# One-column products to other stages, position statistics spread over a panel, and a different order of work at the norms with a shift

## The chip, the cores and the metric

One core of one Trainium2 chip runs the whole program. The metric is the device time of one execution in microseconds (us); lower is better. TensorE (PE in the rows, its weight loads PEld), VectorE (DVE), ScalarE (ACT), GpSimd (POOL) and SyncE (SP, which issues the loads) each run an instruction stream of their own and meet at semaphores.

## The reference, cut to what matters

A transformer on x of 512 positions by 1024 channels, in float32, four layers in all. Two of them belong to a first block whose norms have a scale and a shift made from a condition vector c:

```python
mods = silu(c) @ ada_w[layer] + ada_b[layer]           # 6 blocks of 1024 per layer
sh1, sc1, g1, sh2, sc2, g2 = split(mods, 6)
h = rms_norm(x, norm_mix_g) * (1 + sc1) + sh1
x = x + g1 * (mixer(h) @ w_out)     # layer 0: LRU and stick-breaking; layer 1: 16 heads, window 128
h = rms_norm(x, norm_ffn_g) * (1 + sc2) + sh2
x = x + g2 * ((silu(causal_conv(h @ w_gate)) * (h @ w_up)) @ w_down)
```

The second block (differential attention, a dilated attention of three groups, two squared-relu MLPs) has norms with a gain only; there `rms_norm(x) @ w` is computed as `(x * gain) @ w`, and the factor `1/rms` of each position is applied to the product.

## The kernel before, in words

x lies transposed in `xT` as 8 chunks of 128 channels by 512 positions. Every float32 product of weight and activation is made from three products of rounded parts: high by high, high by low, low by high. A weight tile comes by DMA into `raw`, ACT rounds it into `whi` (`high`, L1641), POOL takes the difference `wlo` (`split`, L873); tile pairs alternate between two buffers. `steps` (L360 to L455) is the list of stages in program order, and each engine's function walks it: "norm", "gemm" (of kinds panel, ffn, relu, down and so on), "window", "stick", "bar", "mods". A unit of a down stage is 8 or 6 channel chunks, so 24 or 18 matmuls of 512 columns, and adds one chunk to `xT` (`down`, L2341 on DVE).

**Modulation sums.** silu(c) @ ada_w needs 12 blocks of 1024 sums. DVE forms, for each block, a 128 by 1024 partial sum over 8 loaded tiles (`ada_add`, L564/L566), and TensorE adds up over the partitions: for each group of 128 columns one matmul whose weights are the partial sum and whose moving operand is a single column of ones (`products`, L1243). These are the one-column products; each shows as two loads and two matmuls in the trace. Blocks 2 to 4 are added up during the stick attention in bursts of 8. Block 5 (the gate of the first ffn) is added up in the down stage behind it, one product after each of 8 units. Blocks 6 to 11 belong to the second layer: in the three down stages of the first ffn one, two and three products follow each of 8 units. The results gather in PSUM columns (`sum_column`) and `modulation` (L2253, L2258) on DVE adds the bias, as the step "mods".

**A norm with a shift.** Three of them follow a down stage (they begin near 300, 688 and 902 us; the very first, at the program's start, is not touched). While the down stage runs, ACT squares each finished chunk (L1787) and DVE adds the square to `sq_sum` (L2201). After the last unit all of PE, ACT and DVE pass a barrier (`bar`); PE keeps busy with 8 matmuls of no use (`keep_rate`, L973), then multiplies `sq_sum` by ones in float32 (L1198), which gives every partition the sum. Twelve more matmuls of no use follow. ACT rounds the weights of the next stage's second unit (in `norm`, ahead of the sum), takes Ln (L1593) and Exp (L1595); DVE scales chunk after chunk (L2455), ACT adds the shift and rounds (L1822), and the first unit of the next stage starts as chunks come in. Ahead of the barrier at 688 ACT also loads a table (L1569).

**Position statistics.** The second block has two fresh norms in front of panels (near 1283 and 1941 us). There each position's sum of squares is wanted on its own partition, in two orders: `token_stats` on TensorE (L1088) multiplies 128 by 128 blocks of `sq_sum` by one column of ones, four blocks that lie together and four whose columns lie four apart. All 8 are issued in one burst after the first of the panel's four rows of work (`l == 0`); ACT reads them (L1709), then DVE.

**Window attention** (`window`, 776 to 857 us) goes head by head: TensorE computes scores (L1345 to L1348), transposes the probabilities (L1356) and adds values (L1367), with heads overlapped.

## Time and profile before

| | |
|---|---|
| median of 3 runs | 2935.57 us (2933.58 to 2941.92) |
| span of the profiled execution | 2940.3 us |
| TensorE matmul busy | 2841.3 us, 97% |
| TensorE weight load busy | 2319.8 us, 79% |
| DVE, ACT, POOL busy | 1744.2, 1222.0, 1077.7 us |
| mean granted TensorE clock | 0.991 |

The rows give a span only, so the profiled execution's own time is known as its span, 2940.3 us, which is 4.7 us above the median. In a timeline row the first number is the start in us, the second the duration; "x8" is the number of instructions merged; the bracket gives idle time just before and what ended it. A clock of 1.00 is 2.4 GHz and 0.50 is 1.2 GHz.

### The profile page before, as it was taken

To read this page: it belongs to the slowest core of one execution; us is meant where nothing else is said; L and a number is where in the kernel's file an instruction comes from. 1 tells how busy PE (TensorE), PEld (TensorE's weight loads), DVE (VectorE), ACT (ScalarE), POOL (GpSimd) and SP (SyncE) were. 2 spreads that over 40 slices of the span, in tenths; PEclk is the share of its full clock that TensorE was granted. 3 is DMA by queue.
4 is the path that set the end of the run, shared out by engine and by line. 5 is a ranking of instruction groups with operands and counts; after the bars stand their busy time and mean duration, and the time that the engine had idled before them with its cause. 6 is when DMAs were issued, how large, how long until landed. Compare 5 with 4: busy or idle time off the path is not lost.

```text
span 2940.3 us, 38997 instructions
## 1 busy us (share of the span) xinstructions
PE 2841.3 (97%) x13385; PEld 2319.8 (79%) x13396; DVE 1744.2 (59%) x2106; ACT 1222.0 (42%) x2059; POOL 1077.7 (37%) x490
## 2 busy tenths in 40 slices
PE   6999999999899999999889999999999999999999
PEld 5767788887677888888658888888888889888887
DVE  7486776776556554668666334557666766544333
ACT  3574432223554322244453222256556665522221
POOL 1312344443213444444314444444422442244443
PEclk9999999999999999999989999999999999999999
DMA  6255263643112333332003333333201330133332
GB/s 217 86 173 185 84 204 98 207 134 91 36 36 79 93 100 93 93 95 87 29 15 93 93 94 98 95 88 94 87 30 52 88 93 30 51 93 93 99 95 93
DMA packets 366012, 278.96 MB, mean 95 GB/s; under 512 B 13490, under 2 KB 321075, under 8 KB 365875
## 3 DMA queue, kind: packets, MB, share of 16 engines
q1 hardware_dynamic: 364624, 276.83, 31.1%
q8 instruction: 82, 1.34, 0.2%
q14 instruction: 55, 0.45, 0.1%
q10 hardware_dynamic: 1251, 0.33, 0.0%
HBM read 275.03 MB, written 2.10 MB: 94 GB/s over the span
## 4 chain that ended last, share of the span: by engine, by line
PE 67%; DVE 3%; ACT 2%; issue 2%; POOL 0%; DVEq 0%; ACTq 0%; POOLq 0%
PE banks L1158 13%; PE banks L1153 12%; PE banks L1162 12%; PE banks L1022 6%; PE banks L1028 6%; PE banks L1025 6%; PE banks L1427 2%; PE banks L995 1%; PE banks L1367 1%; PE banks L1493 1%; PE banks L1155 1%; PE banks L1356 0%; PE banks L1063 0%; PE banks L1400 0%; PE banks L1401 0%
## 5 line engine op out<-in xcount | busy, mean ns | idle before, releaser
L873 POOL TENSOR_TENSOR w_lo<-w_raw,w_hi 128x1024 fp32r<-128x1024 f32 (+1 forms) x423 | 1027.1, 2428 | 1706.8 <-ACT w_hi L1641 1705.8
L1641 ACT ACTIVATE w_hi<-w_raw 128x1024 fp32r<-128x1024 f32 (+1 forms) x424 | 445.6, 1051 | 1131.3 <-PE banks L1162 799.4
L1022 PE MATMUL banks<-w_hi,h_hi 128*128 128x512 f32 x960 | 387.1, 403 | 1.4 <-ACT h_hi L1822 1.4
L1028 PE MATMUL banks<-w_lo,h_hi 128*128 128x512 f32 x960 | 377.3, 393 | 0.7 <-POOL w_lo L873 0.7
L1025 PE MATMUL banks<-w_hi,h_lo 128*128 128x512 f32 x960 | 376.6, 392 | 0.7 <-DVE h_lo L596 0.7
L1153 PE MATMUL banks<-h_hi,w_hi 128*128 128x512 f32 x1280 | 339.0, 393 | 6.7 <-ACT h_hi L1822 6.7
L1158 PE MATMUL banks<-h_lo,w_hi 128*128 128x512 f32 x1280 | 320.8, 391 | 2.5 <-DVE h_lo L596 2.4
L1153 PEld LDWEIGHTS banks<-h_hi,w_hi 128*128 128x128 f32 x1280 | 240.9, 188 | 63.9 <-issue 8.4
L1158 PEld LDWEIGHTS banks<-h_lo,w_hi 128*128 128x128 f32 x1280 | 240.3, 188 | 57.5 <-DVE h_lo L596 8.3
L1162 PE MATMUL banks<-h_hi,w_lo 128*128 128x512 f32 x1152 | 284.5, 389 | 0.0
L1162 PEld LDWEIGHTS banks<-h_hi,w_lo 128*128 128x128 f32 x1152 | 216.2, 188 | 44.9
L1153 PE MATMUL banks<-mid_hi,w_hi 128*128 128x512 f32 x864 | 220.4, 394 | 8.2 <-ACT mid_hi L1774 4.7
L1028 PEld LDWEIGHTS banks<-w_lo,h_hi 128*128 128x128 f32 x960 | 196.7, 205 | 35.5 <-POOL w_lo L873 1.5
L1022 PEld LDWEIGHTS banks<-w_hi,h_hi 128*128 128x128 f32 x960 | 196.7, 205 | 32.8 <-issue 2.1
L1025 PEld LDWEIGHTS banks<-w_hi,h_lo 128*128 128x128 f32 x960 | 197.3, 206 | 31.9 <-DVE h_lo L596 1.0
L1158 PE MATMUL banks<-mid_lo,w_hi 128*128 128x512 f32 x864 | 218.3, 391 | 2.2 <-DVE mid_lo L2321 2.1
L2338 DVE TENSOR_TENSOR xT<-banks,xT 128x512 f32 (+1 forms) x80 | 55.3, 691 | 268.6 <-PE banks L1162 266.8
L1162 PE MATMUL banks<-mid_hi,w_lo 128*128 128x512 f32 x864 | 214.6, 390 | 0.0
L1153 PEld LDWEIGHTS banks<-mid_hi,w_hi 128*128 128x128 f32 x864 | 160.6, 188 | 46.4 <-ACT mid_hi L1774 8.1
L1158 PEld LDWEIGHTS banks<-mid_lo,w_hi 128*128 128x128 f32 x864 | 162.2, 188 | 41.4 <-DVE mid_lo L2321 4.7
L1162 PEld LDWEIGHTS banks<-mid_hi,w_lo 128*128 128x128 f32 x864 | 162.2, 188 | 33.6
L2331 DVE TENSOR_TENSOR mid_lo<-tmp,mid_hi 128x512 f32 (+1 forms) x64 | 123.9, 1936 | 55.6 <-ACT mid_hi L1774 55.6
(364 smaller groups left out, 4260.6 us busy)
## 6 DMA issues: line engine op xcount, KB each, us to landing
Z<-in_ada_w SPq DMA_DIRECT2D x64, 512.0 KB, 5.0
w_raw<-in_m_w_up SPq DMA_DIRECT2D x64, 512.0 KB, 3.9
w_raw<-in_m_w_down SPq DMA_DIRECT2D x64, 512.0 KB, 3.7
w_raw<-in_kv_w SPq DMA_DIRECT2D x48, 512.0 KB, 3.7
w_raw<-in_ffn_w_gate SPq DMA_DIRECT2D x44, 512.0 KB, 3.7
w_raw<-in_ffn_w_up SPq DMA_DIRECT2D x44, 512.0 KB, 3.7
tmp<-in_ada_w SPq DMA_DIRECT2D x32, 512.0 KB, 4.6
w_raw<-in_ffn_w_down SPq DMA_DIRECT2D x32, 512.0 KB, 3.9
```

The lines of the kernel that those rows point to most:

```text
L873: pool.tensor_tensor(wlo[j][:, 0:n], raw[j][:, 0:n], whi[j][:, 0:n], ALU.subtract).then_inc(s_wlo, 1)
L995: mm = pe.transpose(turned(n)[:, j * P:(j + 1) * P], tmp[4 + n % 2][:, j * P:(j + 1) * P], ident)
L1022: pe.matmul(t, hh, wh, start=k == 0, stop=False)
L1025: pe.matmul(t, hl, wh, start=False, stop=False)
L1028: mm = pe.matmul(t, hh, wl, start=False, stop=k == DC - 1)
L1153: pe.matmul(g, whi[par][:, k * P:(k + 1) * P], hi[:, k * S:(k + 1) * S], start=(k == 0), stop=False)
L1158: mm = pe.matmul(g, whi[par][:, k * P:(k + 1) * P], lo[:, k * S:(k + 1) * S], start=False, stop=early and k == st.kc - 1)
L1162: mm = pe.matmul(g, wlo[par][:, k * P:(k + 1) * P], hi[:, k * S:(k + 1) * S], start=False, stop=(k == st.kc - 1))
L1427: mm = pe.matmul(o, dil_vals[:, at:at + P], dil_probs[q % 2][:, own:own + width], start=g == 0 and c == 0, stop=g == 2 and c == NB - 1, sk ...
L1641: act.activation(whi[par][:, 0:kc * P], raw[par][:, 0:kc * P], ACT.Copy).then_inc(s_whi, 1)
L2331: dve.tensor_tensor(ch(mlo, l), tmp[1], ch(mhi, l), ALU.subtract).then_inc(r_lo, 1)
L2338: dve.tensor_tensor(x, G[par], x, ALU.add).then_inc(evac[par], 1)
```

## The change

1. The 8 products of block 5 leave the down stage after the stick attention and go to the norm behind it: each is followed by one matmul of no use, in place of the 12. Their "mods" step moves behind the first ffn stage.
2. The second down stage of the first ffn has one product per unit in place of two, the third none in place of three. Blocks 8 to 11 are added up in the window attention instead, 8 products in a burst ahead of the scores of heads 2, 5, 8 and 11; their "mods" step (3) stands between the window attention and its barrier. DVE's partial sums for blocks 6 to 11 lie in other tiles, since the window uses four of them; the adds themselves stay where they were. Other PSUM columns hold the results.
3. The position statistics are issued two at a time, after each of the four tiles of the second row (`l == 1`). ACT reads them at `l == 2`; DVE makes the head tables first and waits for them after.
4. At the three norms with a shift DVE no longer adds the last square. TensorE multiplies the sum of seven squares by ones behind the first 8 matmuls of no use, and after the barrier adds ones times the last square.
5. At the same norms ACT rounds the weights of the second unit ahead of the barrier and ahead of the last square, in place of after the barrier.

The diff, with context cut:

```diff
@@ -414,12 +414,12 @@
         steps[-1][1].after_stick = True
-        steps[-1][1].products, steps[-1][1].ada = (0, [3]), (0, 8, 8)
-        steps.append(("mods", 1))
+        steps[-1][1].ada = (0, 8, 8)
         ffn(0)
+        steps.insert(next(n for n, (k, st) in enumerate(steps) if k == "gemm" and st.kind == "ffn") + 1, ("mods", 1))
         downs = [st for k, st in steps if k == "gemm" and st.kind == "down" and st.rhs == "mid"]
-        for st, blocks, ada in zip(downs, ([0], [1, 2], [3, 4, 5]), ((8, 16, 8), (24, 16, 8), (40, 8, 4))):
-            st.products, st.ada = (1, blocks), ada
+        for st, blocks, ada in zip(downs, ([0], [1], None), ((8, 16, 8), (24, 16, 8), (40, 8, 4))):
+            st.products, st.ada = blocks and (1, blocks), ada
         steps.append(("mods", 2))
@@ -428,7 +428,7 @@
         panel(od, D, 8, 256, a["od_kn_g"])
-        steps += [("bar", None), ("window", None), ("bar", None)]
+        steps += [("bar", None), ("window", None), ("mods", 3), ("bar", None)]
         gemm_stage("down", 8, DC, a["od_w_out"][0], "y", gate=48 + 16)
@@ -528,7 +528,7 @@
-            t, o = (bank[6], 2 * P) if FIRST * DC <= c < 5 * DC else (bank[7], 0)
+            t, o = (bank[6], 2 * P) if FIRST * DC <= c < 6 * DC else (bank[7], 0) if c < 8 * DC else (bank[4], 0)
             return t[:, o + c:o + c + n]
@@ -537,7 +537,7 @@
         ada_parts = [dict(blocks=range(FIRST, 6), sums=[zt(2 * b, 2) for b in range(4)], ring=[TMP[:, 2 * j * S:(2 * j + 2) * S] for j in range(4)], before=0),
-                     dict(blocks=range(6, 12), sums=[zt(16 + 2 * b, 2) for b in range(6)], ring=[zt(28 + 2 * j, 2) for j in range(4)], before=32)]
+                     dict(blocks=range(6, 12), sums=[zt(16 + 2 * ((b + 4) % 6), 2) for b in range(6)], ring=[zt(28 + 2 * j, 2) for j in range(4)], before=32)]
@@ -555,7 +555,7 @@
             q = ada_parts[part]
-            t = q["sums"][b] if isinstance(b, int) else zt(2 * b, 2)
+            t = q["sums"][b]
             i = DC * b + k
@@ -972,11 +972,14 @@
-            def bar(waits=0):
+            def bar(waits=0, si=None):
                 flush()
                 keep_rate(waits)
+                if si:
+                    pe.wait_ge(n_add, past((DC + 1) * si - 1))
+                    pe.matmul(bank[2], ones, sq_sum, start=True, stop=False).then_inc(n_add, 1)
                 pe.wait_ge(bar_act, nbar[0])
@@ -1032,6 +1035,8 @@
                             turn(before, 0)
+                        if l == 1 and st.norm.raw and st.norm.fresh and st is first_of(st.norm):
+                            token_stats(st.norm, b)
                         if st.first_pair is not None and l in (1, 2):
@@ -1041,8 +1046,6 @@
                         turn(before, l + 1)
-                    if l == 0 and st.norm.raw and st.norm.fresh and st is first_of(st.norm):
-                        token_stats(st.norm)
                 pending[0] = st if st.normed else None
@@ -1080,13 +1083,14 @@
-            def token_stats(norm):
+            def token_stats(norm, b):
                 pe.wait_ge(n_add, past((DC + 1) * norm.sum_index))
-                for k in range(2 * NB):
+                for k in range(2 * b, 2 * b + 2):
                     block = sq_sum[:, k * P:(k + 1) * P] if k < NB else by_class(sq_sum)[:, k - NB, :]
                     mm = pe.matmul(bank[7][:, k:k + 1], block, ones[:, 0:1], start=True, stop=True)
-                mm.then_inc(n_ss, 1)
+                if b == NB - 1:
+                    mm.then_inc(n_ss, 1)
@@ -1194,9 +1198,14 @@
                 if fresh and si > 1 and not norm_list[ni].raw:
-                    pe.wait_ge(n_add, past((DC + 1) * si))
-                    pe.matmul(bank[2], ones, sq_sum, start=True, stop=True).then_inc(n_ss, 1)
-                    keep_rate(12)
+                    pe.wait_ge(n_sq, past(DC * si))
+                    pe.matmul(bank[2], ones, squares[1], start=False, stop=True).then_inc(n_ss, 1)
+                    if si == 2:
+                        for t in range(DC):
+                            products(0, [3], t, 1)
+                            keep_rate(1)
+                    else:
+                        keep_rate(12)
@@ -1338,6 +1347,8 @@
                     pe.wait_ge(e["probs"], past(h - 2))
+                    if h % 3 == 2 and h < 12:
+                        products(1, [2 + h // 3])
                     for b in range(NB):
@@ -1522,7 +1533,10 @@
                     after = steps[at_step + 1] if at_step + 1 < len(steps) else (None, None)
-                    bar(8 if after[0] == "norm" and not norm_list[after[1][0]].raw and at_step else 0)
+                    if after[0] == "norm" and at_step:
+                        bar(8, after[1][1])
+                    else:
+                        bar()
                 elif kind == "norm":
@@ -1571,7 +1585,9 @@
-            def bar():
+            def bar(wide=None):
+                if wide:
+                    high(DC, 1, wide.base + 1, wide.base // 2)
                 if pending[0]:
@@ -1721,7 +1737,7 @@
                         high(kc, 1 - l % 2, st.base + l + 1, (st.base + l + 1) // 2, *following(st, l + 1))
-                    if l == 0 and st.norm.raw and st.norm.fresh and st is first_of(st.norm):
+                    if l == 2 and st.norm.raw and st.norm.fresh and st is first_of(st.norm):
                         if other_tables[0]:
@@ -1812,7 +1828,7 @@
                     return
-                if nxt.early:
+                if nxt.early and ni == 0:
                     high(DC, 1, nxt.base + 1, nxt.base // 2)
@@ -2147,7 +2163,8 @@
                 if kind == "bar":
-                    bar()
+                    after = steps[at_step + 1:at_step + 3]
+                    bar(after[1][1] if at_step and after and after[0][0] == "norm" and after[1][1].early else None)
                 elif kind == "norm":
@@ -2269,8 +2286,10 @@
                     modulation(5, 6, [])
+                elif part == 2:
+                    modulation(6, 8, [(1, 0)])
                 else:
-                    modulation(6, 12, [(1, 0), (1, 1)])
+                    modulation(8, 12, [(1, 1)])
@@ -2341,7 +2360,7 @@
                         raw_low(st.raw_next, l)
-                    if st.squares is not None:
+                    if st.squares is not None and (st.raw_next or not (isinstance(l, int) and l == st.n - 1)):
                         add_square(st.squares, l, par)
@@ -2430,10 +2449,11 @@
                     pending[0] = None
+                if st.normed:
+                    head_tables(st)
                 if st.norm.raw and st.norm.fresh and st is first_of(st.norm):
                 if st.normed:
-                    head_tables(st)
                     for b in range(NB):
```

## Rows read from the trace of the kernel before

**Rows 1.** The page: busy time of each engine, share of the span, instructions.
```profile
PE 2841.3 (97%) x13385; PEld 2319.8 (79%) x13396; DVE 1744.2 (59%) x2106; ACT 1222.0 (42%) x2059; POOL 1077.7 (37%) x490
```
**Rows 2.** Timeline of PE, down stages with one and with two products a unit.
```profile
266.25 0.28 PE L1243 MATMUL banks<-ones_r,Z 128*128 128x1 f32 x2
271.94 0.28 PE L1243 MATMUL banks<-ones_r,Z 128*128 128x1 f32 x2
...
545.67 0.50 PE L1243 MATMUL banks<-ones_r,Z 128*128 128x1 f32 x4
...
551.62 0.50 PE L1243 MATMUL banks<-ones_r,Z 128*128 128x1 f32 x4
```
**Rows 3.** The chain in order of time, a down stage without products.
```profile
866.17 1.81 PE banks L1158 x8
```
**Rows 4.** Timeline, third down stage of the first ffn, three products a unit.
```profile
668.53 4.25 DVE L564 SCALAR_TENSOR_TENSOR Z<-Z,small 128x1024 f32<-128x1024 f32 x2
...
673.49 1.66 PE L1153 MATMUL banks<-mid_hi,w_hi 128*128 128x512 f32 x6 [1.21 <-DVE xT L2341]
...
678.29 1.63 PE L1153 MATMUL banks<-mid_hi,w_hi 128*128 128x512 f32 x6
```
**Rows 5.** Timeline of PE, window attention at its start and in its middle.
```profile
788.46 0.66 PE L1356 MATMUL banks<-squares,tmp 128*128 128x128 f32 x4 [2.67 <-DVE tmp L2590]
...
805.82 0.31 PE L1345 MATMUL banks<-qk_parts 128*128 128x128 f32 x1
...
810.24 0.31 PE L1345 MATMUL banks<-qk_parts 128*128 128x128 f32 x1
```
**Rows 6.** Stretches (us, busy of PE, PEld, DVE, ACT, POOL, clock, DMA): a stick burst.
```profile
192.30:194.10 1.80, 1.72 (x16) 1.75 (x16) 1.45 (x4) 1.76 (x4) 0.00 (x0) 1.00 0.61 150
194.10:198.00 3.90, 3.90 (x25) 3.20 (x25) 3.68 (x5) 3.38 (x8) 0.00 (x0) 1.00 0.29 100
```
**Rows 7.** Timeline of DVE, the modulation step in front of another barrier.
```profile
252.84 0.18 DVE L2253 TENSOR_TENSOR mods<-banks,params 128x24 f32<-128x24 f32 x1
253.06 0.17 DVE L2258 SCALAR_TENSOR_TENSOR norm_scale<-mods,params 128x8 f32<-128x8 f32 x1
```
**Rows 8.** Timeline, the third norm with a shift.
```profile
902.48 0.75 DVE L2341 SCALAR_TENSOR_TENSOR xT<-banks,mods,xT 128x512 f32<-128x512 f32 x1 [1.29 <-PE banks L1162]
...
902.77 1.67 PE L973 MATMUL banks<-mask_b,ident_b 128*128 128x512 bf16 x7 [0.33 <-issue]
903.26 0.63 ACT L1787 ACTIVATE tmp<-xT 128x512 f32<-128x512 f32 x1 [4.58 <-DVE xT L2341]
903.92 0.69 DVE L2201 TENSOR_TENSOR tmp<-tmp 128x512 f32<-128x512 f32 x1 [0.70 <-ACT tmp L1787]
...
904.74 1.06 ACT L1641 ACTIVATE w_hi<-w_raw 128x1024 fp32r<-128x1024 f32 x1 [0.85 <-DVEq L2186]
904.76 1.10 PE L1198 MATMUL banks<-tmp,ones_r 128*128 128x512 f32 x2 [0.32 <-DVEq L2186]
...
905.69 2.75 PE L973 MATMUL banks<-mask_b,ident_b 128*128 128x512 bf16 x12
...
905.87 2.35 POOL L873 TENSOR_TENSOR w_lo<-w_raw,w_hi 128x1024 fp32r<-128x1024 f32 x1 [5.24 <-ACT w_hi L1641]
905.89 0.69 ACT L1593 ACTIVATE tmp<-banks,small 128x512 f32<-128x512 f32 x1
```
**Rows 9.** All of DVE's L2455 in that norm, ns min/median/max.
```profile
L2455 DVE SCALAR_TENSOR_TENSOR tmp<-xT,norm_scale,rstd x8: 737/740/1400, 907.4 to 912.7; 128x512 f32<-128x512 f32 x8
```
**Rows 10.** Timeline of ACT, the norm near 688 us.
```profile
688.89 1.28 ACT L1569 ACT_TABLE_LOAD   x1
```
**Rows 11.** Timeline of PE, the first burst of position statistics.
```profile
1282.64 2.81 PE L1088 MATMUL banks<-ones_r,tmp 128*128 128x1 f32 x16
```
**Rows 12.** Stretches around that burst, columns as in rows 6.
```profile
1282.60:1285.30 2.70, 2.70 (x17) 2.66 (x16) 0.00 (x0) 0.00 (x0) 0.44 (x1) 1.00 0.32 68
1285.30:1289.00 3.70, 3.70 (x10) 2.95 (x11) 0.98 (x5) 1.63 (x4) 1.74 (x1) 0.54 0.28 101
```

## The prediction

> **What bounds the kernel now.** I read the page first: TensorE is busy 97% of the span [rows 1], so most of the time is the number of matmuls times their pitch, and an edit elsewhere counts only where TensorE waits. Then the timeline of each place that the diff touches. About 0.3% (8.8 us) is what a measurement of this kernel can tell from no change.
>
> A plain down unit is three groups of 8 matmuls at 1.81 us, 5.44 us [rows 3]. With one one-column product behind it the period is 271.94 - 266.25 = 5.69, with two 551.62 - 545.67 = 5.95 [rows 2]: a product costs TensorE 0.25 us although its one column is next to nothing. What it costs are weight loads that no long matmul hides.
>
> The burst of 8 position statistics begins at 1282.64 [rows 11] and holds TensorE for 2.7 us. The clock is 1.00 (2.4 GHz) in it and falls to 0.54, mostly the 1.2 GHz level, for the 3.7 us behind it [rows 12]; TensorE had streamed almost no columns for 2.7 us though its record says busy. The second burst, at 1941 us, does the same.
>
> At a norm with a shift TensorE waits for a chain: last square on ACT, its add on DVE, the float32 sum, Ln, Exp, then DVE's first scaled chunk. That first chunk takes 1400 ns where the others take 740 [rows 9], and POOL's split of the second weight tile runs from 905.87 to 908.22, over its first half [rows 8]. DVE starts a chunk each 0.66 us, so about 0.66 us is lost there.
>
> **Products out of the down stages.** Down stage behind the stick attention: 7 periods shrink by 0.25, -1.75 us (the eighth product lies behind the last unit, in the norm). Second down stage: 8 x (5.95 - 5.69) = -2.1. DVE carries two partial sums a unit there as it does in the first down stage, whose period with one product is 5.69 as well, so it allows that. Third: three products cost a period of 678.29 - 673.49 = 4.80 against 4.08 for 18 matmuls (three quarters of 5.44). But TensorE does not set the pace of the first units: DVE takes 4.25 us for two adds, and TensorE waits 1.21 us for it at 673.49 [rows 4]. That wait grows by what the products leave, so only the units behind it gain: two full periods, 2 x 0.7 = -1.4, not 5.6. No range below 0 for these three; -1.4 could be -3 if DVE's wait is shorter than it looks.
>
> **Products into the window attention.** A stick burst of 8 takes 1.8 us, at clock 1.00 in and behind it [rows 6]. In the middle of the window attention a head starts each 810.24 - 805.82 = 4.42 us with no idle time between its matmuls [rows 5], so three of the four bursts are bought in full: 3 x 1.85 = +5.6. The first, ahead of head 2, meets TensorE's idle 2.67 us before 788.46 [rows 5]. But DVE takes the maxima of head 2 before it scales head 0, which that wait is for, so I charge 0.4. Sum +6.0; bounds 0 (if heads are paced by ACT and DVE after all) and 8.2 (four bursts of 2.05).
>
> **The modulation steps.** The one between window and barrier is two small DVE instructions behind the last output, 252.84 to 253.23 where they stand in the same place now [rows 7]: +0.4, 0 to 0.6. TensorE, ACT and POOL all wait at that barrier. The step behind the first ffn stage costs the same 0.4 on DVE with a down stage's partial sums queued behind it; they have 0.4 us slack in every unit of 5.69, so 0. The one at 688 us gets shorter but stands behind a table load. The new place of DVE's sums costs nothing.
>
> **The three norms.** In the third norm [rows 8] the 8 filler matmuls end their stream near 904.3, and the sum starts at 904.76 because DVE's add ends at 904.61. After the change the sum of seven starts at 904.3. A float32 multiplication by 512 columns occupies TensorE until 905.69, 0.93 us, of which 0.85 is stream, so the second starts at 905.15 and its result is out at 906.25, against 905.86 now. The removed add of 0.69 is replaced by a second pass of 0.85: Ln starts **later** by 0.35. ACT's rounding of 1.06 us now stands ahead of the last square, which ends near 904.2 and not 903.9; that is still early enough. What gains is the split on POOL: it follows the rounding, ends near 906.0, before DVE's first chunk, which gets its 0.66 us back. Net -0.3. The first norm is alike, and its barrier starts 0.1 us earlier with no product in front: -0.4. Its 8 products with 8 fillers take 8 x (0.25 + 0.21) = 3.7 us where 12 fillers took 2.6, which may outlast the wait of TensorE by 0.5; chunks come in each 0.66 us and take 0.45, so it catches up. In the second norm ACT's table load of 1.28 [rows 10] stands between the square and the barrier, so rounding before the square delays it by 1.06 - 0.75 = 0.3, where 0.75 is DVE's update of the chunk [rows 8] that the square waits for anyway; with the 0.7 back at its first chunk, -0.4. Sum -1.1, bounds -3 and +1.5. The earlier split also lets SP issue the following load 2 us sooner; nothing waits for it.
>
> **The position statistics.** The same 8 products cost the same loads in pairs, 2.4 us net, give or take 0.5. What I expect back is the clock: in the 3.7 us behind the burst nine matmuls start (the tenth of that row is the burst's last) [rows 12], where at 1.81 us for 8 [rows 3] they would take 2.04: -1.7, twice, -3.4. Each pair has 6 matmuls of 512 columns on either side. ACT and DVE have two more rows of work before they need the result: 0.
>
> Here the Trainium skill speaks against the change. TensorE: Matmul & The Clock Gate, What's actually happening, has the clock fall after an idle stretch, and this burst is not idle by the record; by that rule pairs would bring back nothing, and the sum would be 0. I go by the trace, where both bursts are followed by the fall.
>
> **Sum:** -1.75 - 2.1 - 1.4 + 6.0 + 0.4 - 1.1 - 3.4 = **-3.4 us** (0.11%). On the profiled span 2940.3 becomes 2936.9; on the median of the runs, 2935.57, which is 4.7 us below that execution, it gives **2932.2**. The change says products move off the critical path; by my count they mostly move from one TensorE-bound stage into another.
>
> **Rivals.**
> - *The bursts in the window pull the clock down.* Place: the scores of heads 2, 5, 8 and 11, narrow matmuls of 128 and 256 columns. For it: 2.7 us of such products did so twice. Against it: three stick bursts of 1.8 us did not. Price up to 1.7 each, 4 x 1.7 = +6.8: 2939.0, slower than before by 3.4 us. It decides as soon as three of the four do it.
> - *The window hides the bursts*, because softmax on ACT and DVE and not TensorE sets the head's period. Against it: no idle TensorE between 801 and 817 us. It gives back 5.6: 2926.6, faster by 9.0.
> - *The fall of the clock has another cause*, and pairs do not prevent it. Then 3.4 is not gained: 2935.6.
> - *The norms do not gain*: POOL is not what slows DVE's first chunk. Then 2.0 us go: 2934.2.
>
> **How the numbers follow.** Forecast 0.45, clock falling in the window 0.12, window hides 0.15, clock not coming back 0.15, norms 0.13. All but the second rival lie within 8.8 us of before by their centres. That one sits on the edge, so half its chance, with a little for gains that add up (the third down stage at -3, norms at -3), is faster by over 0.3%: 0.11. Slower by over 0.3% needs the clock to fall at low levels for long: 0.04. The range reaches from the hidden window, less run-to-run spread, to the clock falling in it: 2925.5 to 2939.0.
>
> **What would show it.** In the new profile: down periods of 5.44, 5.69 and, in the last units of the third, 4.08; a gap of 1.8 us between heads where products stand in the window, and its whole length 6 us more; Ln after the end of the down stage not earlier than now (3.45 us in the third norm); DVE's first L2455 at 0.74 us, not 1.40; a clock of 1.00 around 1285 and 1943 us. I am wrong if the window keeps its length, if the clock still falls in the panels, or if Ln comes earlier by more than 0.3 us.

## The result and the profile after

The changed kernel takes 2942.66 us (median of 20 runs, 2937.05 to 2949.76), the kernel before 2940.1 us beside it (20 runs): ratio 1.0013, 95% interval [1.0007, 1.0019], so 3.8 us slower. Run again with other kernels it gave 1.0014 [1.0002, 1.0025]. Predicted were 3.4 us less and a range that ends at 2939.0. The sign was wrong. The measured time lies 3.7 us above the range, but the prediction counted from 2935.57, the median of 3 runs of the kernel before, and 20 runs put that kernel at 2940.1: 4.5 us of the 10.5 between 2932.2 and 2942.66 are the low start.

The pair of profiled executions goes the other way, 2940.3 to 2937.1 us of span, so neither may be read by its total. First the stages whose rows came out near the prediction. Timeline of the changed kernel, with the start, the length, what ran, and in brackets the idle time before it: first and second down stage, third down stage, end of the down stage ahead of the third norm and that norm.

```profile
261.84 1.98 PE L1157 MATMUL banks<-y_hi,w_hi 128*128 128x512 f32 x8
...
267.28 1.98 PE L1157 MATMUL banks<-y_hi,w_hi 128*128 128x512 f32 x8
...
544.65 0.28 PE L1252 MATMUL banks<-ones_r,Z 128*128 128x1 f32 x2
...
550.34 0.28 PE L1252 MATMUL banks<-ones_r,Z 128*128 128x1 f32 x2
...
663.47 1.66 PE L1157 MATMUL banks<-mid_hi,w_hi 128*128 128x512 f32 x6 [1.41 <-DVE xT L2360]
...
670.34 1.65 PE L1157 MATMUL banks<-mid_hi,w_hi 128*128 128x512 f32 x6 [2.48 <-DVE xT L2360]
...
905.92 1.97 PE L1166 MATMUL banks<-y_hi,w_lo 128*128 128x512 f32 x8
...
909.12 2.35 POOL L873 TENSOR_TENSOR w_lo<-w_raw,w_hi 128x1024 fp32r<-128x1024 f32 x1 [3.03 <-ACT w_hi L1657]
...
909.74 1.02 PE L982 MATMUL banks<-tmp,ones_r 128*128 128x512 f32 x2
...
910.60 1.02 PE L1202 MATMUL banks<-tmp,ones_r 128*128 128x512 f32 x2
...
911.74 0.69 ACT L1609 ACTIVATE tmp<-banks,small 128x512 f32<-128x512 f32 x1 [2.17 <-PE banks L1202]
```

The first down period is 5.44 and no longer 5.69, the second 5.69 and no longer 5.95 [rows 2]. In the third, DVE makes TensorE wait longer (1.41, 2.48 us against 1.21 [rows 4]) and takes back most of what the products leave. In the third norm Ln (at 911.74) begins 3.85 us after the last matmul of the down stage (905.92 + 1.97), where it was 3.45: later by 0.4, as predicted. The first scaled chunk of DVE takes what the others do. All eight, ns min/median/max:

```profile
L2475 DVE SCALAR_TENSOR_TENSOR tmp<-xT,norm_scale,rstd x8: 743/744/752, 913.2 to 917.9; 128x512 f32<-128x512 f32 x8
```

It was 737/740/1400 [rows 9]. POOL's split now ends at 911.5 us, ahead of DVE's first chunk at 913.2. In every profile with the norm part the first chunk takes 0.75 us at all three norms, in every profile without it 1.39 to 1.55.

Then the window attention. Its stage, from the first matmul of the panels to the first of the down stage behind it, as a view of one stretch (us and busy time of PE, PEld, DVE, ACT, POOL, then the granted clock, the DMA share and GB/s), of the kernel before and of the changed one:

```profile
695.34:858.63 163.29, 144.77 (x824) 115.11 (x825) 99.53 (x185) 91.42 (x267) 36.83 (x23) 0.97 0.13 40
```

```profile
690.29:862.48 172.19, 154.88 (x888) 124.33 (x889) 99.79 (x187) 91.88 (x267) 36.82 (x23) 0.95 0.12 35
```

8.9 us longer for 64 more instructions of TensorE (32 products, two passes each), where 6.4 were predicted (6.0 for the bursts, 0.4 for the step), and the clock is lower. Around the last two of the four bursts, in front of heads 8 and 11, and at the start of the down stage behind, the changed kernel shows:

```profile
802.73 1.84 PE L1252 MATMUL banks<-ones_r,Z 128*128 128x1 f32 x16
...
820.27 1.84 PE L1252 MATMUL banks<-ones_r,Z 128*128 128x1 f32 x16
```

```profile
802.20:805.60 3.40, 3.40 (x31) 3.32 (x30) 1.80 (x6) 2.50 (x10) 0.00 (x0) 1.00 0.00 0
805.60:809.00 3.40, 3.40 (x14) 2.43 (x13) 1.38 (x3) 1.01 (x2) 0.00 (x0) 0.50 0.00 0
809.00:812.40 3.40, 3.40 (x27) 2.80 (x26) 1.57 (x5) 2.27 (x8) 0.00 (x0) 1.00 0.02 5
819.30:822.70 3.40, 2.92 (x26) 2.88 (x26) 3.29 (x9) 2.50 (x10) 0.00 (x0) 1.00 0.56 154
822.70:826.10 3.40, 3.40 (x16) 2.75 (x15) 1.95 (x4) 0.57 (x3) 0.00 (x0) 0.50 0.00 0
...
863.60:867.00 3.40, 3.40 (x10) 2.63 (x9) 0.00 (x0) 0.00 (x0) 2.36 (x1) 0.50 0.00 0
```

Behind each of the two bursts the clock is 0.50 (1.2 GHz) for 3.4 us, in which half the work is done. Such a stretch is called a fall of the clock below, and it costs 1.7 us. One more lies at 863.6 in the down stage. None of the three lies in the trace of before. Without the two, the window stage costs 8.9 - 3.4 = 5.5 us, a little under the predicted 6.4.

Why the pair's totals mislead: the differential attention, which the change does not touch. The last 107.4 us of it, ahead of the down stage behind, in the kernel before and in the changed one (columns as above):

```profile
1430.03:1537.43 107.40, 87.65 (x432) 59.81 (x432) 75.59 (x159) 59.87 (x175) 16.48 (x17) 0.89 0.04 11
```

```profile
1427.79:1535.19 107.40, 87.80 (x452) 60.46 (x451) 79.59 (x168) 62.35 (x182) 21.17 (x26) 0.94 0.04 11
```

The profiled execution of before had an unlucky pass there, clock 0.89 against 0.94, and shows 20 matmuls fewer in the same time. From the first panel to the down stage behind, the stages differ by 7.4 us, and only 1.5 of them belong to the statistics (below).

### The profile page after: what moved, and what is told of

The parts are those of the page before. It is cut to its first block, busy times and chain, and to the rows that moved or that the text cites. A ratio compares the mean times of both kernels' runs of the same rounds, so it can differ in the third digit from the quotient of the medians.

```text
span 2937.1 us, 39025 instructions
## 1 busy us (share of the span) xinstructions
PE 2839.3 (97%) x13387; PEld 2319.3 (79%) x13398; DVE 1744.4 (59%) x2104; ACT 1222.3 (42%) x2059; POOL 1077.8 (37%) x490
## 4 chain that ended last, share of the span: by engine, by line
PE 67%; DVE 3%; ACT 2%; issue 2%; POOL 0%; DVEq 0%; ACTq 0%; POOLq 0%
PE banks L1162 13%; PE banks L1157 12%; PE banks L1166 12%; PE banks L1025 6%; PE banks L1031 6%; PE banks L1028 6%; PE banks L1438 2%; PE banks L998 1%; PE banks L1378 1%; PE banks L1159 1%; PE banks L1504 1%; PE banks L1367 1%; PE banks L1066 0%; PE banks L1411 0%; PE banks L1413 0%
## 5 line engine op out<-in xcount | busy, mean ns | idle before, releaser
L2445 DVE TENSOR_TENSOR tmp<-tmp,head_sums 128x512 f32<-128x512 f32 (+1 forms) x84 | 135.2, 1609 | 35.3 <-issue 23.2
```

The source lines that it names most:

```text
L2445: dve.tensor_tensor(by_head(tmp[4 + n % 2], w), roped, scale, ALU.mult).then_inc(h_out, 1)
```

## The experiments

There are 18 runs of 16 new kernels and the changed one, each timed in 5 rounds beside the kernel before on the same chip. A ratio of 0.001 is 2.9 us. A mean clock is the average over the clocks listed for a kernel's runs.

**The parts one by one, and the change without its window part.** The first kernel spreads the statistics alone:

```diff
+                        if l == 1 and st.norm.raw and st.norm.fresh and st is first_of(st.norm):
+                            token_stats(st.norm, b)
...
-                for k in range(2 * NB):
+                for k in range(2 * b, 2 * b + 2):
```

> The kernel before with one part of the change: position statistics in pairs behind the matmuls of a later row. By the account of the parts this is worth -3.4 us, two falls of the clock of 1.7 us each; the granted clock is 1.00 from 1283 to 1289 us and behind the second pairs near 1941 us. Theory 'window clock' (the change loses by clock falls at its window bursts): -3.4 here. Rival 'falls are not to be had' (the clock falls somewhere else instead, so that its mean stays): 0, within 1 us, and the mean granted clock is that of before.

The second holds only the moved window products and their step (diff as in the change), the third only the norm part, the fourth is the changed kernel with

```diff
-        for st, blocks, ada in zip(downs, ([0], [1], None), ...
+        for st, blocks, ada in zip(downs, ([0], [1, 2], [3, 4, 5]), ...
...
-                    if h % 3 == 2 and h < 12:
-                        products(1, [2 + h // 3])
```

> The kernel before with one part of the change: the products of blocks 8 to 11 in four bursts in the window attention, with the modulation step behind it. Theory 'window clock': -2.1 and -1.4 us in the two down stages, +6.4 in the window, which is +2.9, and on top of it 1.7 us for each fall of the clock in and behind the window, two to four of them as in the changed kernel's trace: +6 to +10, mean clock lower than before by 0.001 to 0.002. Rival 'price alone': +2.9, clock as before. Rival 'noise in the differential attention': +2.9 and falls that come and go there in both kernels.

> The kernel before with one part of the change: last square to TensorE and the rounding of the weights ahead of the barrier, at the three norms with a shift; the products stay where they are. Theory 'window clock' with the predicted parts: -1.1 us, the third norm shorter by 0.35 as in the pair of profiles. Rival 'norms lose' (the second pass over 512 columns and the late split cost more than they give): +0.5 to +1.5.

> The changed kernel with the products of blocks 8 to 11 and their modulation step put back into the second and third down stages; the rest of the change stays. Theory 'window clock': -1.75 (down stage behind the stick attention) -1.1 (norms) -3.4 (statistics) = -6.3 us against before, so faster than both kernels. Rival 'falls are not to be had': -2.9. Rival 'norms lose': -4 to -5.

Measured: statistics 0.9989 [0.998, 0.9998], window part 1.0032 [1.0021, 1.0043], norms 0.9992 [0.9981, 1.0002], change without window part 0.9994 [0.9985, 1.0003]. The window part alone is 9.4 us slower (6.2 to 12.6), at the upper end of what the clock theory allowed, and the mean clock is 0.9894 against 0.9919 of before. Its stage (columns as above):

```profile
694.36:872.01 177.65, 160.32 (x888) 128.46 (x889) 99.87 (x187) 91.79 (x267) 36.83 (x23) 0.92 0.12 37
```

But the change without it gains 1.8 us and not 6.3: either more sizes are wrong, or clock is lost elsewhere too.

The statistics alone were 3.2 us faster, with an interval (0.6 to 5.9) that holds the predicted 3.4 and much less; their size is read from the stages. They gain 1.5 us at the first place and 0.65 at the second. From the first matmul of the panels to the 192nd the kernel before takes 1326.80 - 1276.83 = 49.97 us and the changed one 1330.49 - 1282.01 = 48.48; at the second place 1985.01 - 1935.34 = 49.67 and 1981.70 - 1932.67 = 49.03. The other kernels' profiles give the same within 0.06 us, but for one (gap_fill) that is 1 us longer at the second place. The second place of the changed kernel:

```profile
1939.59 0.50 PE L1031 MATMUL banks<-w_lo,h_hi 128*128 128x512 f32 x1 [0.86 <-POOL w_lo L873]
...
1940.62 0.50 PE L1091 MATMUL banks<-ones_r,tmp 128*128 128x1 f32 x4
...
1942.45 0.50 PE L1091 MATMUL banks<-ones_r,tmp 128*128 128x1 f32 x4
...
1944.30 0.86 PE L1091 MATMUL banks<-ones_r,tmp 128*128 128x1 f32 x4
...
1946.50 0.86 PE L1091 MATMUL banks<-ones_r,tmp 128*128 128x1 f32 x4
```

The first two pairs take 0.50 us, the last two, whose columns are picked by class, 0.86: together the 2.7 us of the burst, as predicted. But ahead of them TensorE waits 0.86 us for POOL's low part of the next weights. The burst of before stood two matmuls ahead of this wait and covered it. At the first place no such wait shows. So it is 1.5 at the one and 1.5 - 0.86 = 0.65 at the other.

**What a burst costs: columns or time.** Four bursts of constants are added to the kernel before, once as 8 one-column products and once as 8 matmuls of 512 columns; a third kernel cuts the changed kernel's bursts in pairs; a fourth puts them into TensorE's wait ahead of the window.

```diff
+                    if h % 3 == 2 and h < 12:
+                        for t in range(DC):
+                            pe.matmul(bank[4][:, 64 + t:65 + t], ident, ones[:, 0:1], start=True, stop=True)
```

```diff
+                            pe.matmul(bank[4], identb[:, :], maskb[:, 0:S], start=True, stop=True)
```

```diff
                     for b in range(NB):
+                        if h % 3 == 2 and h < 12:
+                            products(1, [2 + h // 3], 2 * b, 2)
```

```diff
                         turn(pending[0], b)
+                        if moved:
+                            first, last = moved[b:b + 2]
+                            products(1, [2, 3, 4, 5], first, last - first)
```

> The kernel before, with four bursts of 8 one-column products of a constant added in the window attention, at the heads where the change puts its bursts; nothing else differs, so this prices the bursts alone. Theory 'window clock': 3 x 1.85 + 0.4 = +6.0 us of TensorE's time and 1.7 us for each fall of the clock that they bring, two to four: +9 to +13, mean clock 0.001 to 0.002 below before. Rival 'price alone': +6, clock as before. Rival 'the window hides them': 0 to +2.

> As extra_bursts, with 8 matmuls of 512 columns in place of each burst: about the same time of TensorE (8 x 0.226 = 1.8 us) but full of columns. Theory 'window clock': +6 us and no further falls of the clock, so 3 to 7 us less than extra_bursts; mean clock as before or above it. Rivals 'price alone' and 'the window hides them': the same time as extra_bursts.

> The changed kernel with each window burst cut into four pairs, one ahead of the scores of each block of 128 rows in the same heads; the same 32 products. Theory 'window clock', in the form that the length of the burst is what counts: the falls go, mean clock up by 0.001, 3 us less than the changed kernel, about as before. In the form that the columns of a longer stretch count: the narrow matmuls between the pairs (128 and 256 columns) do not save the clock, and the time is the changed kernel's within 1 us. Rival 'price alone': the same time as the changed kernel.

> The changed kernel with all 32 products of the window bursts put between the last transposes of the panels and the first scores of the window attention, where the changed kernel's TensorE waits 0.81, 1.63, 1.62 and 4.79 us: 3, 6, 6 and 17 products of 0.25 us. The clock is low there anyway. Theory 'window clock': the bursts' 6 us and their falls are gone, at most 2 us come back because the products run at the low clock: 6 to 9 us below the changed kernel, 3 to 6 below before. Rival 'price alone': 4 to 6 below the changed kernel. Rival 'falls come elsewhere': no gain beyond 3.

Measured: extra_bursts 1.002 [1.001, 1.003], extra_wide 1.0022 [1.0014, 1.0031], spread_pairs 1.0004 [0.9995, 1.0014], gap_products 1.0003 [0.9994, 1.0011]. Four bursts cost their time, and the window does not hide them: +5.9 us (2.9 to 8.8) and +6.5. That speaks for 'price alone', since the columns did not make extra_bursts slower. In the profiles the two differ by the clock all the same, 0.95 and 0.97 in the window stage, the kernel with one-column bursts first:

```profile
694.61:866.54 171.93, 154.88 (x889) 124.33 (x889) 99.67 (x185) 91.89 (x267) 36.86 (x23) 0.95 0.13 38
```

```profile
694.73:863.72 168.99, 151.77 (x853) 118.87 (x857) 99.67 (x185) 91.78 (x267) 36.84 (x23) 0.97 0.13 38
```

Pairs bring the changed kernel from 1.0013 to 1.0004, with a clock of 0.97 in the stage (169.50 us). The intervals overlap, so by the times this is likely and not shown.

The falls themselves say more than the mean clock of the stage, which is 0.95 also in three profiles without a single product in the stage (stats_only, norms_only, stats_norms_again). All six profiles with whole bursts (extra_bursts and the five with the change's window part) have 6.8 us of low clock that begins behind 800 us, within the heads and right at the end of the third or the fourth burst. None of the fourteen others has any there, extra_wide and spread_pairs among them. Ahead of 800 us, between 788 and 797, falls come with bursts (4 of 6) and without (5 of 14).

gap_products gained 3 us on the changed kernel and not 6 to 9. In the low clock ahead of the window a product costs 0.43 us (7.25 us for 17), and these 17, the last ones, stood ahead of the barrier's signal, so ACT, DVE and then POOL came late:

```profile
771.52 7.25 PE L1255 MATMUL banks<-ones_r,Z 128*128 128x1 f32 x34
783.04 0.45 PE L1357 MATMUL banks<-qk_parts 128*128 128x128 f32 x1 [4.26 <-POOL qk_parts L863]
```

**The fifth block, the two parts that gain, a better gap, and the change once more.** move5_only holds only the move of block 5's products into the first norm, stats_norms both gaining parts, gap_fill this:

```diff
-        for st, blocks, ada in zip(downs, ([0], [1], None), ...
+        for st, blocks, ada in zip(downs, ([0], [1, 2], [3]), ...
...
+            def pairs(first, last):
+                for i in range(first, last):
+                    products(1, [4, 5], i, 1)
+                    keep_rate(1)
```

> The kernel before with one part of the change: the 8 products of block 5 out of the down stage behind the stick attention and into the wait of the first norm, each followed by a filler matmul, and their modulation step behind the first stage of the ffn. The two kernels so far that hold this move together with the statistics and the norms (the changed one and the one without the window part) come out 3 to 5 us above the sum of the parts. Theory 'sum of parts': -1.75 us, clock as before. Rival 'the move costs clock' (pairs of one product and one filler carry too few columns behind a barrier, and the clock falls at the start of the next stage, as it does at 318.8 us in the kernel without the window part, for 1.6 us): 0 to +2, mean clock 0.001 below before.

> The kernel before with the statistics part and the norms part together, all products of the modulation where they were. The two alone gave ratios of 0.9989 and 0.9992. Theory 'sum of parts': -4.5 us by the predicted sizes, -5.6 by the two ratios, so faster than both kernels by 0.15 to 0.2%. Rival 'the parts do not add' (whatever falls of the clock the one avoids come elsewhere): -1 to -2.

> The changed kernel without window bursts: the products of blocks 8 and 9 go back to the second and third down stage (8 in each), those of blocks 10 and 11 go where TensorE waits between the panels and the window attention, each followed by a filler matmul of 512 columns, the last 9 pairs behind the signal of the barrier. In gap_products the clock was low for 17.1 us there and 17 products took 7.25 us ahead of that signal, so that ACT and DVE came late. Theory: against the changed kernel -5.5 (bursts) -1.7 to -3.4 (falls at them) -1.9 (no low clock at the window's start) +2.0 (second down stage) +0 to +2 (third): -5 to -8 us, 2 to 5 below before. Rival 'the gap is not free' (what is put in it delays the first scores as it did in gap_products): within 2 us of the changed kernel.

> The changed kernel once more, beside the others of this call, so that they can be compared with it on the same chip: the theory that the window part outweighs the rest says +2 to +5 us against before and a mean clock 0.001 to 0.002 lower, as in its first 20 runs. If it comes out at or below before, the first comparison was a matter of that chip.

Measured: move5_only 1.0 [0.9989, 1.001], stats_norms 0.9994 [0.9984, 1.0004], gap_fill 0.9996 [0.9985, 1.0006], after_again 1.0014 [1.0002, 1.0025]. The move into the norm gains its 1.8 us in the stage, and in 4 of the 9 profiled kernels that hold it the clock falls in the ffn stage behind, in none of those without it. The change without its window part shows this:

```profile
312.00:315.40 3.40, 3.35 (x11) 1.55 (x10) 3.40 (x6) 3.02 (x4) 0.00 (x0) 1.00 0.00 0
315.40:318.80 3.40, 2.58 (x7) 1.12 (x7) 2.88 (x5) 0.00 (x0) 0.00 (x0) 1.00 0.00 0
318.80:322.20 3.40, 3.40 (x10) 2.63 (x10) 2.91 (x2) 1.06 (x1) 2.19 (x1) 0.50 0.00 0
```

gap_fill kept the clock up ahead of the window, and in its profile it then fell in the heads, where TensorE has work:

```profile
770.00:775.00 5.00, 3.52 (x31) 3.27 (x30) 1.89 (x3) 1.36 (x3) 4.69 (x6) 1.00 0.01 3
...
784.00:794.20 10.20, 9.21 (x43) 8.28 (x43) 6.93 (x17) 6.00 (x22) 0.00 (x0) 0.50 0.00 1
```

Before, TensorE is busy for 4.95 of the 10.2 us of low clock in this place (770.4 to 780.6), here for 9.21.

**Is it the position?** Fillers that do nothing, ahead of the second ffn stage of layer 0, move all that follows against the falls before it:

```diff
+                    if st.kind == "ffn" and st.layer == 0 and st.first == PARTS[1][0]:
+                        keep_rate(8)
```

> The changed kernel with 4 filler matmuls of 512 columns (0.9 us, TensorE busy and full of columns) ahead of the second ffn stage of layer 0, where nothing waits; they do no work, they only move all that follows by 0.9 us against the clock's ups and downs before it. Theory 'window clock, each burst for itself': +0.9 us against the changed kernel, mean clock as there. Rival 'position': whether a stretch of few columns brings the clock down hangs on when it comes after the earlier falls, so a shift changes how many falls follow: a difference of more than 2 us either way from +0.9.

> As after_delay4 with 8 filler matmuls, 1.8 us. 'Each burst for itself': +1.8 us against the changed kernel. 'Position': off that by more than 2 us; if it comes out faster than the changed kernel, time that does nothing has paid for itself.

> The kernel before with 4 filler matmuls (0.9 us) at the same place. 'Each burst for itself': +0.9 us against before. 'Position': off that by more than 2 us, in one at least of the two delays.

> The kernel before with 8 filler matmuls (1.8 us) at the same place. 'Each burst for itself': +1.8 us against before. 'Position': off that by more than 2 us, in one at least of the two delays.

Measured against before: after_delay4 1.0016 [1.0007, 1.0024], after_delay8 1.0023 [1.0013, 1.0033], before_delay4 1.0006 [0.9995, 1.0016], before_delay8 1.0013 [1.0002, 1.0025]. With 1.0014 for the changed kernel, four fillers add 0.6 and 1.8 us, eight 2.6 and 3.8, for prices of 0.9 and 1.8. None is off its price by more than 2.0 us, the bound set ahead (before_delay8 sits on it), but each interval is some 3 us wide to either side: the position theory is not borne out, and not excluded. Their worth lies in their profiles. Changed kernel with 4 fillers:

```profile
695.56:871.54 175.98, 158.67 (x889) 127.39 (x889) 99.95 (x187) 91.78 (x267) 36.85 (x23) 0.93 0.12 34
```

The window stage of the five profiled kernels with the change's window part takes 172.19, 175.10, 175.98, 175.94 and 177.65 us, on average 175.4; that of the nine with no work added in it 163.29, 166.02, 164.71, 163.34, 164.93, 163.30, 166.10, 164.49 and 164.93, on average 164.6. The longest without is shorter than the shortest with. The window part costs 10.8 us there. Of these 5.5 are TensorE's time and 5.3 the clock; 3.4 of the 5.3 are the falls that begin behind 800 us.

The same comparison takes a gain away. The third down stage with the norm behind it is 2.2 us shorter in the first pair of profiles (48.21 to 46.00), but not so in the others. 0.5 of the 2.2 is the norm's (7.92 to 7.43 us from the end of the down stage's last matmul to the first of the panels; 7.42 to 7.55 in every profile with the norm part). The down stage alone takes 39.7 us on average in the five profiles and 40.3 in the nine: 0.6 us gained and not 1.7. In five of the seven profiles of kernels that have all products out of it the clock falls there, in both of those that have a part out, and in one of the eleven that have them all in. In window_only the fall follows a stretch in which TensorE waits for DVE:

```profile
669.30:672.70 3.40, 0.71 (x4) 0.39 (x3) 2.73 (x3) 0.35 (x1) 0.00 (x0) 0.98 0.49 138
672.70:676.10 3.40, 3.40 (x10) 2.66 (x9) 2.23 (x3) 1.65 (x3) 1.83 (x1) 0.51 0.00 0
```

**Two last kernels.** stats_norms once more, and with it one block of 8 products moved from the third down stage behind the barrier's signal:

```diff
                 pe.drain().then_inc(bar_pe, 1)
                 keep_rate(waits)
+                if moved:
+                    products(1, moved)
```

> Statistics and norms together once more. Its stages against before, where no random fall lies, add up to -3.1 us (-0.3 first norm, -0.4 second, -0.3 third, -1.5 and -0.6 in the panels); its first 12 runs gave -0.7 by the means, give or take 1.2. Theory 'stage sums hold': -3, so a ratio of 0.9990. Rival 'something that the profile does not show takes it back': 0 within 1 us.

> Statistics and norms, and of the moved products only the last block of 8: out of the third down stage, into the 4.79 us wait of TensorE ahead of the window attention, behind the signal of the barrier, so that ACT and DVE don't wait for it; its modulation step stands behind the window. The other products stay where they were. Expected against stats_norms: -1 to -2 in the third down stage (DVE sets its pace at 4.25 us a unit), 0 for the 8 products (3.4 us at the low clock in 4.79 us of waiting), +0.4 for the step: -1, and no falls of the clock in the heads; -4 against before. Rival 'the gap is not free', as in gap_fill, where its stage came out 2.4 us longer: 0 to +2 against stats_norms.

Measured: stats_norms_again 0.9988 [0.998, 0.9997], one_in_gap 0.9992 [0.9983, 1.0]. The stage sums hold in the second sample of stats_norms. Its two samples, 0.9994 and 0.9988, have a mean of 0.9991, 2.6 us faster than before and 6 us faster than the change: of the kernels tried, the one to keep. The block in the gap brought nothing that can be told on top; its window stage is 166.21 us.

## Why the prediction was wrong

Point by point, in us against before:

| Step | predicted | measured |
|---|---|---|
| down stage behind stick attention and first norm | -2.15 | -2.1 in the stage, +1.6 in 4 of 9 profiles behind it |
| second down stage | -2.1 | -2.0 |
| third down stage and second norm | -1.8 | -2.2 in the first pair, -1.1 over the profiles |
| window attention with its step | +6.4 | +10.8: 5.5 and falls of the clock |
| third norm | -0.3 | -0.3 |
| position statistics, both places | -3.4 | -1.5 and -0.65 |

**The step that failed is the window's.** TensorE's time for bursts and step was nearly right (5.5 for 6.4; 5.9 us for the bursts in extra_bursts). Left out of the sum was the clock, which I had as the first rival at a chance of 0.12 with a price of at most 6.8 us and a time of 2939.0. That rival took place, at 10.8 - 5.5 = 5.3 us. That its 3.4 us slower lies so near the measured 3.8 is in part luck: its price was too high, and other terms came out short. My evidence against it was that three stick bursts had no fall behind them [rows 6]. That was one execution. In the profile of the kernel that spreads the statistics, the same burst, at 194.66 us, is followed by

```profile
194.60:198.00 3.40, 3.33 (x26) 3.01 (x26) 2.97 (x6) 2.95 (x6) 0.00 (x0) 1.00 0.56 171
198.00:201.40 3.40, 3.40 (x13) 2.85 (x12) 3.14 (x4) 3.24 (x8) 0.00 (x0) 0.50 0.39 101
```

and another at 216.70 by a fall at 218.5. What comes and goes from run to run has a rate, and three cases of one trace don't give it. Over all twenty profiles, in all of which this stage has the same work, 11 of 60 stick bursts are followed by a fall, in 6 of the profiles. I should have put the likeliest number of falls into the sum, about half of the price.

What is shown is that the change's window part brings falls, and that in the profiles those behind 800 us come with whole bursts (6 of 6) and not with wide matmuls, with pairs or with neither (0 of 14). That the few columns of the bursts are the reason is the likeliest reading, but the runs' times of extra_bursts and extra_wide do not differ by the 3.4 us that it asks for, so it is not settled. Nor is it explained why the change's products cost more there, 10.8 us by the stages, than the bursts of constants, 5.9 us by the runs (2.9 to 8.8): apart from the step of 0.4, they differ in the numbers multiplied and in where the partial sums lie, and no run takes these apart.

**The statistics were mis-sized by 1.25 us.** The clock part held to the letter: all eight profiled kernels with bursts show the fall behind both, none of the twelve with pairs does. The Trainium skill, TensorE: Matmul & The Clock Gate, What's actually happening, has the clock fall after an idle stretch; here TensorE's record says busy for 2.70 of 2.70 us [rows 12] and the clock falls behind it, and with pairs it does not, so the measurement decides. But I expected 1.7 us at each place and got 1.5 and 0.65: I had not asked what the burst covered. At the second place it covered 0.86 us of POOL, and the wait took its place.

**The rest.** The norms behaved as predicted, POOL's split and DVE's first chunk included (the prediction's own times for the end of the sum, 906.25 and 905.86, differ by 0.39 where it says 0.35; measured 0.4); 'the norms do not gain' and 'the window hides the bursts' are out. The third down stage was taken at -1.4: the wait for DVE was seen, but not that the clock falls behind longer waits, and -0.6 is left. The sum by the measured column is -2.1 - 2.0 - 1.1 + 10.8 - 0.3 - 2.15 = +3.15. With 4/9 x 1.6 = 0.7 behind the first norm, and 1.2 for a fall in the down or ffn stage behind the window (1.4 to 1.6 us in four of those five profiles, in none of the nine others), it is about +5. The ratios say +3.8 (2.1 to 5.6) and +4.1 (0.6 to 7.4), so the sum is a little high, but inside both. The change without its window part fits badly: -2.1 - 0.4 - 0.3 - 2.15 + 0.7 = -4.25, just inside the interval of the measured -1.8 (-4.4 to +0.9).

## What to carry to other kernels

Ask of each place to which small matmuls are moved whether TensorE waits there, and how wide the matmuls around them are: a burst costs its own time wherever TensorE is busy, and among the window's narrow matmuls the change lost about as much again in clock. Ask too what the products covered where they stood: taken away, they left a wait of 0.86 us at one place and longer waits with a fall of the clock behind them at another. Spread such products among wide matmuls, or leave them there. Where the clock varies from run to run, compare stages over several profiles and totals over many runs; one pair of profiles had the sign of this change wrong.

## What the runs showed of the hardware

- The granted clock falls to 0.50 for 3.4 us although TensorE's record was busy for 2.92 to 3.40 of the 3.40 us ahead of it, where one-column products ran in them. Which burst it follows changes from run to run: 11 of 60 in the stick stage. The times of the 159 runs of the kernel before that stand beside the experiments reach from 2933.7 to 2948.4 us, with listed clocks from 0.994 to 0.988.
- A one-column product costs 0.25 us at full clock and 0.43 at the low one. A pair of products whose weight columns are picked at a stride takes 0.86 and not 0.50 us.
- Fillers in a wait can move the low clock instead of removing it: 10.2 us with TensorE busy for 4.95 of them became 10.2 us with it busy for 9.21, in the one profile of gap_fill.
- DVE's first scaled chunk took 1400 ns while POOL's split ran and 752 ns with the split ahead of it.
